# Forgetting attention with the keys' decays added by VectorE, together with two joined changes

## The reference, cut to what matters

```python
def forgetting_attention(q, k, v, log_f):
    c = jnp.cumsum(log_f, axis=1).transpose(0, 2, 1)      # one decay per head and position
    ...
        logits = jnp.einsum('bqhd,bkhd->bhqk', qi, k).astype(jnp.float32) * scale
        logits = logits + ci[..., :, None] - c[:, :, None, :]
        logits = jnp.where(mask, logits, NEG_INF)
        probs = jax.nn.softmax(logits, axis=-1).astype(v.dtype)
```

## Time and profile before

| | us |
|---|---|
| median of 3 runs | 3681.6 (3678.24 to 3692.95) |
| the profiled execution | 3690.24 |
| its span, first to last instruction | 3688.4 |
| TensorE busy | 3442.1 (93%) |
| VectorE busy | 1201.6 (33%) |
| ScalarE busy | 909.1 (25%) |
| GpSimd busy | 188.2 (5%) |

### The profile page before, as it was taken

How to read it: one execution, slowest core, us unless ns; L and a number is a source line. 1 busy time by engine, 2 the same in 40 slices (tenths; PEclk the granted TensorE clock), 3 DMA queues, 4 the chain that set the end, 5 groups by cost and what they waited for, 6 DMA issues and landing times.

```text
span 3688.4 us, 44443 instructions
## 1 busy us (share of the span) xinstructions
PE 3442.1 (93%) x18510; PEld 1935.6 (52%) x18510; DVE 1201.6 (33%) x2623; ACT 909.1 (25%) x1709; POOL 188.2 (5%) x210
## 2 busy tenths in 40 slices
PE   8999999999999999998999988979989999887899
PEld 4464454754465454754755766533325656663333
DVE  1323451022323461022343388130002335663011
ACT  1344130111344130113233322031113234221110
POOL 0000000000000000000000133000000000320000
PEclk9999999999999999999999999989999999888899
DMA  4211172312111172312101000159982110013897
GB/s 151 80 58 49 49 298 74 118 43 68 57 58 46 57 290 71 119 49 93 35 29 46 1 2 30 57 196 368 354 302 99 41 41 24 1 41 143 333 409 312
DMA packets 119477, 432.56 MB, mean 117 GB/s; under 512 B 13040, under 2 KB 15216, under 8 KB 118896
## 3 DMA queue, kind: packets, MB, share of 16 engines
q1 hardware_dynamic: 112896, 406.66, 29.9%
q0 software_dynamic: 6384, 23.07, 1.9%
HBM read 417.10 MB, written 12.58 MB: 116 GB/s over the span
## 4 chain that ended last, share of the span: by engine, by line
PE 85%; DVE 7%; DMA 4%; ACT 2%; issue 2%; POOL 0%; SPq 0%; DVEq 0%; ACTq 0%; POOLq 0%
PE bank L1647 82%; DMA ring<-in_stream 2%; PE bank L1762 1%; DVE work L1381 1%; PE bank L764 0%; DMA h_sb<-in_stream 0%; ACT work L2009 0%; DVE work L2167 0%; DVE work L2169 0%; DVE work L1451 0%; DVE levels L1381 0%; DMA work<-in_stream 0%; DVE small L1450 0%; PE bank L1834 0%; DMA work<-tokens,slot_tok 0%
## 5 line engine op out<-in xcount | busy, mean ns | idle before, releaser
L1647 PE MATMUL bank<-h_sb,ring 128*128 128x512 f32 (+2 forms) x3200 | 1254.3, 549 | 25.1 <-ACT h_sb L987 8.2
L1647 PEld LDWEIGHTS bank<-h_sb,ring 128*128 128x128 f32 (+1 forms) x3200 | 592.5, 190 | 585.0 <-issue 542.2
L1647 PE MATMUL bank<-y_sb,ring 128*128 128x512 f32 (+1 forms) x1152 | 474.9, 573 | 9.7 <-DVEq L212 9.7
L1647 PEld LDWEIGHTS bank<-y_sb,ring 128*128 128x128 f32 x1152 | 219.4, 191 | 260.2 <-issue 245.5
L1647 PE MATMUL bank<-work 128*64 128x128 f32 (+7 forms) x2016 | 292.5, 347 | 26.8 <-DVE small L2174 11.8
L1969 ACT ACTIVATE work<-bank 128x512 f32<-128x512 f32 (+1 forms) x256 | 129.7, 517 | 755.3 <-PE bank L1647 646.5
L1647 PE MATMUL bank<-ring,h_sb 128*128 128x128 f32 (+2 forms) x2144 | 286.4, 313 | 1.4 <-ACT work L1102 0.7
L1647 PEld LDWEIGHTS bank<-ring,h_sb 128*128 128x128 f32 (+2 forms) x2144 | 232.4, 186 | 43.9 <-issue 40.6
L1647 PEld LDWEIGHTS bank<-work 64*128 64x128 f32 (+2 forms) x2016 | 184.1, 170 | 115.3 <-issue 77.0
L1647 PE MATMUL bank<-ring,work 128*64 128x512 f32 (+1 forms) x800 | 212.5, 603 | 2.8 <-DMA ring<-in_stream 2.2
L1647 PE MATMUL bank<-y_sb,work 128*64 128x128 f32 (+2 forms) x920 | 170.7, 437 | 0.6 <-DMA work<-in_stream 0.3
(11 more groups left out here) (303 smaller groups left out, 3539.4 us busy)
## 6 DMA issues: line engine op xcount, KB each, us to landing
ring<-in_stream SPq DMA_DIRECT2D x578, 512.0 KB, 5.6
y_sb<-in_stream SPq DMA_DIRECT2D x110, 512.0 KB, 6.9
h_sb<-in_stream SPq DMA_DIRECT2D x40, 512.0 KB, 14.8
work<-in_stream SPq DMA_DIRECT2D x20, 512.0 KB, 15.2
work<-in_bias SPq DMA_DIRECT2D x2, 2688.0 KB, 9.1
tokens<-work POOLq DMA_DIRECT2D x10, 512.0 KB, 4.7
x_sb<-in_xT SPq DMA_DIRECT2D x4, 512.0 KB, 6.3
sums<-y_sb POOLq DMA_DIRECT2D x4, 512.0 KB, 5.2
```

The lines of the kernel that those rows point to most:

```text
L1647: return nc.tensor.matmul(o, a, b, start=first, stop=last, skip_group_check=True)
```

## The change

1. The second matmul step of the forgetting units is gone. The decays of the keys of all 8 heads are stored to memory and loaded back so that each partition holds the rows (`forget_rows`), two heads while the sliding-window attention still runs, six into the room of its operands when it has ended. VectorE adds the row to the scores in the pass that makes the maximum; the exponential reads the result from SBUF. The banks are freed by VectorE.
2. `decays` is a generator in three slices, one after each of the units 5, 6 and 7; its second copy of 8 rows, the copies and the four multiplies are gone.
3. The 12 small matmuls of the state-space part stand ahead of the wait for `operand_ready`.
4. The HGRN key multiply of passes 1 to 5 moves from VectorE to GpSimd, behind the differences of level 1.
5. In the experts the first one-hot transposes stand ahead of `turn_rows`; the sums begin when the half of the outputs that they read is there, and in layer 0 all context parts come before the wait for `sums_in`.

```diff
-        decay_of = [flat(10240, T), flat(10752, T), levels_sb[:, 0:T], levels_sb[:, T:2 * T]]
-        def fox_units():
+        forget_rows = [tiles(10240, 2, T), tiles(0, 6, T)]
+        def fox_units(l):
...
-                        steps = [(half, 0, n, q[r, t, qi], k[r, t, 0:n]),
-                                 (half, 0, n, decay_of[t][r, qi], decay_keys[r, 0:n])]
-                        subs.append(dict(steps=steps, diagonal=qi))
+                        row = forget_rows[0][:, hh, 0:n] if hh < 2 else forget_rows[1][:, hh - 2, 0:n]
+                        subs.append(dict(steps=[(half, 0, n, q[r, t, qi], k[r, t, 0:n])], diagonal=qi, row=row,
+                                         ready=forget_in[t] if i == 0 and t < 2 and half == 0 else None, layer=l))
...
-                    yield dict(subs=subs, nk=n, banks=(0, 1), freer="exp", outs=[outs], slots=1, closes=i == 3, gate=4 + t)
+                    yield dict(subs=subs, nk=n, banks=(0, 1), freer="dve", outs=[outs], slots=1, closes=i == 3, gate=4 + t)
...
-                        if f == 0:
-                            pe.wait_ge(freed_by_act, written)
+                        if f % 4 == 0:
+                            pe.wait_ge(freed_by_act, written[f // 4])
...
                 slot_tokens()
+                transpose_one_hots(0)
                 at["gathered"] = turn_rows()
                 pe.wait_ge(freed_by_act, at["gathered"])
-                expert_pass(("gate", 0), expert_input(0), 4, "act", lambda r: transpose_one_hots(0) if r == 2 else None)
+                expert_pass(("gate", 0), expert_input(0), 4, "act")
...
-                all_read("act")
+                pe.wait_ge(freed_by_act, written[0])
+                for f in range(KT):
+                    fs = slice(f * P, (f + 1) * P)
+                    if f == 4:
+                        pe.wait_ge(freed_by_act, written[1])
+                    b = 2 * (f % 2) + 1
+                    claim(b, "dve")
+                    for q in range(N_QUADS):
+                        ins = mm(banks[b][:, 0:CTX], out_c[:, q, fs], spread_c[q], q == 0, q == N_QUADS - 1)
+                    ins.then_inc(full_for_dve, 1)
                 pe.wait_ge(sums_in, 16)
...
-                            if ci == 1:
-                                keys(i + 1)
...
+            for l in range(DEPTH):
+                pool.wait_ge(forget_made, l + 1)
+                V.dma_start(forget, decay_keys[0:8, :]).then_inc(forget_stored, 16)
+                pool.wait_ge(forget_stored, 16 * (l + 1))
+                everywhere = lambda v, n: v.rearrange("(a h) t -> a h t", a=1).to_broadcast([P, n, T])
+                V.dma_start(forget_rows[0], everywhere(forget[0:2, :], 2)).then_inc(forget_in[0], 16)
+                pool.wait_ge(swa_done, l + 1)
+                V.dma_start(forget_rows[1], everywhere(forget[2:8, :], 6)).then_inc(forget_in[1], 16)
...
                         me.link(level_difference(V, l, i, n), differences_ready, wait=False)
+                        if n == 1:
+                            p, d = PASSES[i]
+                            pool.wait_ge(key_exp_ready, 5 * l + i)
+                            me.link(V.tensor_tensor(k_exp, k_exp, hg_z[:, 3 * d + p, :], ALU.mult), operand_ready, wait=False)
...
-                pe.wait_ge(operand_ready, me.nth(operand_ready))
                 id16 = const[FD, C_IDENT + 32:C_IDENT + 48]
...
                 ins.then_inc(full_for_dve, 1)
+                pe.wait_ge(operand_ready, me.nth(operand_ready))
...
+                            elif "row" in sub:
+                                block = banks[s][:, sub["diagonal"]]
+                                me.link(V.tensor_tensor(block, block, cst(C_CAUSAL), ALU.add))
+                                if sub["ready"] is not None:
+                                    dve.wait_ge(sub["ready"], 16 * (sub["layer"] + 1))
+                                me.link(V.tensor_tensor_reduce(scores_in(i, s)[:, 0:nk], banks[s][:, 0:nk], sub["row"], -1.0,
+                                                               POS_BIG, ALU.add, ALU.min, m), freed_by_dve)
+                                me.notify(max_ready)
...
-                    if between is not None and i == 5:
-                        between()
+                    if between is not None and i >= 5:
+                        next(between, None)
...
-                attention(swa_units(l), scores_in, decays)
+                attention(swa_units(l), scores_in, decays())
                 me.notify(operand_ready)
-                attention(fox_units(), scores_in)
+                me.notify(swa_done)
+                attention(fox_units(l), scores_in)
```

More of the change, by code:

```diff
@@ L120, in build @@
         zeros_made = sem("zeros_made")
+        forget_made = sem("forget_made")
+        forget_stored = sem("forget_stored")
+        forget_in = [sem(f"forget_in{n}") for n in range(2)]
+        swa_done = sem("swa_done")
         zeros_stored = sem("zeros_stored")
@@ L131, in build @@
         keys_read = sem("keys_read")
+        key_exp_ready = sem("key_exp_ready")
         levels_read = sem("levels_read")
@@ L865, in experts @@
                     pe.wait_ge(freed_by_act, at["hidden"])
+                    written = []
                     for half in range(2):
                         expert_pass((f"down{half}", q), expert_hidden, 2, "act")
+                        written.append(freed["act"])
                     if not both:
-                        at["scatter"] = scatter(q, freed["act"])
+                        at["scatter"] = scatter(q, written)
                 if not both:
@@ L883, in experts @@
                         ins = mm(banks[b][:, j * P:(j + 1) * P], sums_tok[:, j, fs], ident, False, j == CHUNKS - 1)
[L884 to L887, removed]
                     ins.then_inc(full_for_dve, 1)
@@ L1035, in exponentials @@
                 difference()
-                me.link(A(k_exp, k_exp, ACT.Exp), act_output, wait=False)
+                me.link(A(k_exp, k_exp, ACT.Exp), key_exp_ready if i else act_output, wait=False)
                 for n in range(7):
@@ L1531, in experts @@
                 if both:
-                    add_gated(l, 5, lambda n: 2 * (n % 2), both)
+                    for s in (1, 0):
+                        for n in range(KT):
+                            bank_full()
+                            o = x[:, n, SPANS[s]]
+                            me.link(V.scalar_tensor_tensor(out=o, in0=banks[2 * (n % 2) + s][:, 0:(T, CTX)[s]],
+                                                           scalar=modc(l, 5, n, s), in1=o, op0=ALU.mult, op1=ALU.add),
+                                    freed_by_dve)
+                            if s == 0 and n % 2:
+                                me.notify(act_input)
             def second_layer(l):
@@ L2064, in first_layer @@
                     act.wait_ge(zeros_stored, 16 * CHUNKS)
-                attention(fox_units(), scores_in, turned,
+                attention(fox_units(l), scores_in, turned,
                           lambda n: evacuate(y[:, 8 + n, :], banks[2 + n % 2][:, :], ACT.Silu), 8, 2)
@@ L2177, in attention @@
                                 me.notify(max_ready)
-                            else:
-                                if "diagonal" in sub:
-                                    block = banks[s][:, sub["diagonal"]]
-                                    me.link(V.tensor_tensor(block, block, cst(C_CAUSAL), ALU.add))
+                            elif "row" in sub:
[6 more added lines that the diff above has]
+                                me.notify(max_ready)
+                            else:
                                 me.link(V.reduce_max(m, banks[s][:, 0:nk], AX.X, negate=True), max_ready, wait=False)
@@ L2228, in decays @@
                     await_(act_output)
-                    for rows in (slice(0, 8), slice(64, 72)):
-                        me.link(V.scalar_tensor_tensor(out=gates[rows, :], in0=gates[rows, :], scalar=0.0, in1=gtmp[rows, :],
-                                                       op0=ALU.min, op1=ALU.subtract))
-                        me.link(V.tensor_tensor_scan(decay_all[rows, :], gates[rows, :], gates[rows, :], 0.0, ALU.add,
-                                                     ALU.bypass))
-                        me.link(V.tensor_scalar(decay_keys[rows, :], decay_all[rows, :], -1.0, None, ALU.mult))
-                        of_queries = slice(rows.start + 32, rows.stop + 32)
-                        me.link(V.tensor_copy(decay_all[of_queries, :], decay_all[rows, :]))
-                        me.link(V.memset(decay_all[rows, :], 1.0))
-                    for t in range(4):
-                        me.link(V.tensor_scalar(decay_of[t], decay_all, const[:, C_DECAY + t:C_DECAY + t + 1], None, ALU.mult))
+                    rows = slice(0, 8)
+                    me.link(V.scalar_tensor_tensor(out=gates[rows, :], in0=gates[rows, :], scalar=0.0, in1=gtmp[rows, :],
```

(5 more changed lines are left out.)

6 lines of the change are left out of this document (4 added, 2 removed).

## The result

The changed kernel takes 3643.6 us (median, 3640.2 to 3647.6), 0.9875 of the kernel before beside it (95% interval 0.9855 to 0.9895): 1.25% faster, where 1.16% was forecast. Four executions of the kernel before, taken beside it, have a median of 3687.3 us (3678.2 to 3693.8), 43.7 above; the 3681.6 that the forecast starts from is the median of three of them. The profiled execution took 3644.4 us, its span 3642.6; against the span before, 45.8 us less, where the sum said 42.6.

A forecast was written before the change was run, and what follows sets the result against it. TensorE, busy 93% of the span, was taken as the bound, with waits for VectorE in the HGRN. Terms -17.2 - 11.8 - 5.0 - 11.0 + 3.5 - 1.1 = -42.6 us, off the median 3681.6: 3639 us, range 3624 to 3656.

The forecast's parts named there:

- Part 1: Forgetting attention: second score matmul removed, -17.2 us over both layers, all on the path; VectorE's extra work costs 0.
- The slack that I leaned on: Forgetting stage, last unit: probabilities scaled at 341.48, transposed at 342.30; 0.8 us to absorb probabilities about 0.5 us later.
- Part 2: Sliding-window stage: decays in three slices close TensorE's stalls, -11.8 us; the granted clock no longer falls, -5.0 us.
- the cover: Part 2: slice and pass under 4 us, bank wanted after 8.5; Part 3: 20 us for the second load.
- Part 3: Decay rows loaded into all partitions by DMA: second load takes 8 to 15 us, covered, cost 0.
- Part 4: State-space part: token sums run inside the wait for the last convolution, -11.0 us (-8.8 to -11.6).
- Part 5: HGRN key multiply to GpSimd: layer 0 about -2.5, layer 1 +6.0, together +3.5 us (-4.3 to +8).
- Rival A: HGRN: key multiply falls into GpSimd's shadow, -4.3 for +3.5 us, whole 3631; chance 0.18.
- Part 6: Experts: last sum begins earlier, one-hot transposes move under a wait, -1.1 us (0 to -2).
- B: Shorter forgetting stage loses its slack, by late probabilities or a broadcast: +14 us, 3653; chance 0.10.
- C: Second broadcast of decay rows served by few DMA engines: 86 us in two layers, 3725; chance 0.05.
- D: Sliding-window stage: the stall only moves and the clock falls as before, +12 to +17 us, 3654; chance 0.07.

## Why the prediction was right, point by point

- **Part 1, -17.2: right.** The step put back cost 17.1 in the two forgetting stages and 17.9 to the state sums; the forgetting stage ran in 90.1 us where 90.2 was written. VectorE's extra work was over-sized: 10 us per layer were estimated, its busy time in the stage rose from 39.5 to 41.2. The slack that I leaned on was real but is thinner: the last unit's probabilities are scaled by 324.9 and transposed at 325.40, 0.5 us later, where it was 0.8.
- **Part 2, -11.8 - 5.0: right in sum, with one reason that decides nothing.** The stage lost 17.0. The old block put back gave 15.3, as the clock's part varies (3.2 there, 5.2 in the kernel before). I derived the cover from the slices; one block of the shortened decays fits too, with 0.4 us to spare. What the slices alone would have done to the old block stays open.
- **Part 3, 0: right.** The landing was 7.0 us, below my 8 to 15; the cover is 24 us, not 20, since I ended it at the masking and not where TensorE wants the bank.
- **Part 4, -11.0: right, slightly low.** The move back cost 12.0.
- **Part 5, +3.5: the sign is not supported.** The step that failed is layer 0's size: "such a gap goes ... about -2.5". Each product has two waits of TensorE, for its third and for its fourth bank, and I took only one. In passes 0, 1 and 3 they were 1.6, 1.1 (with one under 0.3) and 1.8 us, and all went; in pass 2 they were these:

```profile
2183.07 1.77 PE L1647 MATMUL bank<-ring 64*128 64x128 f32 x18 [2.12 <-DVE work L1381]
2185.50 1.00 PE L1647 MATMUL bank<-ring 64*128 64x128 f32 x5 [0.65 <-DVE work L1381]
```

and after only one, 0.3 us longer than the two (pass 4 was alike, but there two more waits, 0.34 and 0.71, went):

```profile
2137.14 3.42 PE L1680 MATMUL bank<-ring 64*128 64x128 f32 x23 [3.10 <-DVE work L1395]
```

Layer 0's waits fell from 23.4 to 18.5, 4.9 us. Layer 1 was right in its mechanism: +1.04 for the 1.2 written at the wait for the product in four of the five passes (+0.49 in the first), waits up by 5.6 in all for the 6.0 written. GpSimd's multiply was under-sized, 1.98 to 1.99 us there for the 1.47 taken from the difference of the same width. By waits the part is +0.7, in the two profiled executions +1.1, and over all executions the stretches average -8.8 and +3.4, -5.4 in sum. That -8.8 holds the clock, 0.95 to 0.98 in three executions of one and ten of the other, so I put part 5 between -5 and +1, by these figures. Rival A's size (-4.3) lies in it, by another way than A's: layer 0 gained more, layer 1 did lose. Why layer 1's 5.6 us of waits made its stretch only 4.1 longer isn't settled. The rule of the Trainium skill, SBUF — State Buffer, section "Who interferes with whom", is borne out by the 2.02 beside the 1.99: VectorE's half, 0.83 where the multiply stands elsewhere, ended 0.27 us behind GpSimd's multiply.
- **Part 6, -1.1: the size stays open.** The -3.4 of the table is inside what the same code moves by. Of the transposes, layer 1's gave about 1 where I had counted 0.5, taking that layer as bound by its weight stream; layer 0's isn't clear of the noise. The sums' step wasn't tried by itself.
- **Rivals.** B, C and D are excluded by the runs named. A is half right.

The whole came out 4.6 us above the forecast of 3639, although the change gained more than written: 45.8 us between the two profiled executions, 43.7 between the medians of four, for 42.6. That is the starting point, 3681.6 where the four executions give 3687.3. The range of the whole was wide enough to hide part 5: by the averages that part lies 9 us below what was written, so the agreement of the whole doesn't support its sum term by term; the runs do that, for parts 1 to 4.

## What to carry to other kernels

Price a move to another engine by the place where the operation lands, beside which of the first engine's operations, and not by the engine alone: the same multiply behind level 1 cost layer 1 some 3 us and behind level 3 gained 2.6 (172.3 to 169.7). Count every wait behind an operation, also the short second one. When a change removes work and also cuts up what is left, ask which of the two closes the stall.

## What the runs showed of the hardware

- One load of 1536 KB from 12 KB of memory into all 128 partitions lands in 7.0 us; five in a row came 6.8 to 7.5 us apart in layer 0 and 6.8 to 8.4 in layer 1. That is 225 GB/s (1536 KB in 7.0 us), half again the 146 GB/s of the load of the sums.
- GpSimd's multiply of 128 x 768 took 1.99 us beside VectorE's halves of the first level and 1.81 beside predicated copies and the start of the next level; VectorE's took 0.99.
- A stretch with equal waits to 0.1 us took 363.7 or 368.5 us, by the granted clock (0.98 or 0.96). A difference under 5 us in this stage needs several executions or a count of the waits.
